# Scan chunk 0 prepared in the last input tile, squares of two chunks added on VectorE, three final additions on POOL

## The chip, the core and the metric

One NeuronCore of a Trainium2 chip. The kernel is one launch; its time is the device time of that launch in microseconds. The engines work side by side and meet only through semaphores: TensorE (PE, matmuls into PSUM), VectorE (DVE), ScalarE (ACT), GpSimd (POOL) and SyncE (SP, which issues the DMAs). An engine takes its instructions in the order written, and one that waits holds up all behind it.

## What is computed

The reference is one layer of a streaming encoder on 1024 prompt tokens and 64 sample tokens (T = 1088 columns), width 1024. A combined projection feeds two head groups: latent attention (8 heads) and an RWKV-7 scan (8 heads, state of 64 x 64 per head). Their outputs are projected together, and a SwiGLU of width 2816 follows. Cut to what the change touches:

```python
def rms_norm(x, g):
    return x * lax.rsqrt(jnp.mean(x * x, axis=-1, keepdims=True) + RMS_EPS) * g

proj = h @ lw['w_in']                          # c_q, c_kv, k_r, rw
q = rms_norm(c_q, lw['q_norm_g']) @ lw['w_uq']
ckv_new = rms_norm(c_kv, lw['kv_norm_g'])
...                                            # attention; scan over r, decay, k, v, kk, a
m = jnp.concatenate([o_attn, o_rw], axis=-1) @ lw['w_out']
x = x + gt_a * rms_norm(m, lw['norm_g'][1])
h = rms_norm(x, lw['norm_g'][2]) * (1 + sc_f) + sh_f
f = (jax.nn.silu(h @ lw['w_gate']) * (h @ lw['w_up'])) @ lw['w_down']
x = x + gt_f * rms_norm(f, lw['norm_g'][3])
```

## The kernel before

Features lie on the 128 partitions, tokens on the free axis, so a row of 1024 features is 8 tiles. The tokens are cut into three chunks `CH` of 364, 364 and 360 columns; the output projection takes them in `OUT_ORDER` = 1, 0, 2. Large projections run as three reduced-precision products (`chunk_product`, L440); attention, scan and norm sums are plain float32. Each engine has its own program, an order written out by hand. Four stages follow one another: input projection (to about 350 us), attention interleaved with the scan (to about 1010), output projection with two norms per chunk (to about 1190), and feed-forward with its final norm.

A norm is split over the engines. ScalarE squares (`norm_squares`, two pieces of four tiles), TensorE adds the eight tiles of squares by eight matmuls with a matrix of ones (`norm_sum`, L478), ScalarE takes the root (`norm_root`, L489), VectorE the reciprocal (`norm_recip`, L495).

**Seam of input projection and attention.** The last input tiles are the latents `ckv` and `cq`. VectorE norms them chunk by chunk (`latent_norm`, L1482), three times "kv", then three times "q". The scan runs over 17 chunks of 64 tokens. A chunk is first prepared: SP loads it (`load_chunk`), VectorE makes running sums of the log decay (`prepare_sums`, L1531), ScalarE their exponentials and a copy (`prepare_scalar`), VectorE two operands of products (`prepare_rows`, L1543 to L1546), POOL the third (`prepare`, L820). Then TensorE multiplies (`products`, L1977), VectorE masks (`causal`, L1554), TensorE transposes (`turns`), and an inversion in six levels follows. `interleave` mixes these slots with the units of attention (`keys`, `query`, `scores`, ...) in a fixed ratio: keys group 0, products, keys group 1, transposes, keys 2 and 3, first level, and so on. The working tiles of chunk 0 (`cum`, `pinc0`, `bk`, ...) share memory with the weight tiles of the input projection, so its preparation comes after the last input matmul. `products` of chunk 0 also waits for the last query root.

**Output projection.** `out_tile(t, n)` makes 16 half-width groups of matmuls for tile n of the t-th chunk (L2241); ScalarE evicts it (`put_m`, L1259). While chunk t is projected, chunk t-1 goes through norm "m", the residual addition (`residual`, L1728 and L1732), norm "n2" and the modulation with its split in two parts (`feed` on VectorE, `affine_split` on ScalarE). TensorE adds the "m" squares behind tile n = 0 and the "n2" squares behind n = 4. `OUT_PARTS` says behind which eviction ScalarE takes the root of n2 and the split.

**End.** Per chunk, ScalarE squares, scales 8 or 16 pieces by the gain (L1375) and takes the root; VectorE (`finish`) multiplies a half by the reciprocal root (L1855) and adds it to x (L1856), half by half. SP stores each half.

Of the kernel before, what the change touches and what calls it, by code (L numbers as in the profile page):

```python
# [21 lines left out]
P = 128  # L22
# [28 lines left out]
OUT_ORDER = [1, 0, 2]  # L51
LEVELS = 6
Y_EARLY = 12
OUT_PARTS = {3: "n2 root", 7: "split"}
# [143 lines left out]
def build(nc, d):  # L198
    with ExitStack() as ctx:
# [3 lines left out]
        def place(start, *tensors):  # L203
# [49 lines left out]
        cum, pinc0, pneg, bk, ar0, vv, gm0, tt0, xt, bktm0, uv, st0, st1, rhs, end = place(  # L253
            WA, ("cum", [P, PAIRS, C + 1]), ("pinc0", [P, PAIRS, C + 1]), ("pneg", [P, PAIRS, C]), ("bk", [P, PAIRS, 2 * C]),
            ("ar0", [P, PAIRS, 2 * C]), ("vv", [P, PAIRS, 2, C]), ("gm0", [P, 2, PAIRS, 2 * C]),
            ("tt0", [P, 2, PAIRS, C]),
            ("xt", [P, PAIRS, C]), ("bktm0", [P, PAIRS, P]), ("uv", [P, PAIRS, P]), ("st0", [P, PAIRS, DH]), ("st1", [P, PAIRS, DH]),
            ("rhs", [P, PAIRS, C]))
# [14 lines left out]
        ci0, ci1, yb0, yb1, vz0, vz1, ar1, bktm1, pr0, pr1, spr, pt, pinc1, aw, end = place(  # L273
            MIX_AT, ("ci0", [P, SF, PAIRS, C]), ("ci1", [P, SF, PAIRS, C]), ("yb0", [P, PAIRS, C]), ("yb1", [P, PAIRS, C]),
            ("vz0", [P, PAIRS, P]), ("vz1", [P, PAIRS, P]), ("ar1", [P, PAIRS, 2 * C]), ("bktm1", [P, PAIRS, P]),
# [8 lines left out]
        yt, x2a, x2b, s0, s1, m1, *w_late, end = place(  # L284
            R2, ("yt", [P, KR, T]), ("x2_0", [P, KD, 364]), ("x2_1", [P, KD, 364]), ("sq2_0", sq), ("sq2_1", sq), ("m1", [P, KD, 364]),
            ("wo5", tile), ("wo6", tile), ("wo7", tile))
        x2, sq2 = [x2a, x2b], [s0, s1]
# [50 lines left out]
        root_ready, rstd_ready = sem("root_ready"), sem("rstd_ready")  # L338
# [41 lines left out]
        x3_in, scaled, y_done, stored = sem("x3_in"), sem("scaled"), sem("y_done"), sem("stored")  # L380
# [88 lines left out]
        def norm_sum(pe, name, sqbuf, c):  # L469
            k, _ = NORMS[name]  # L470
            n, q = CH[c][1], norm_no[name, c]
            if q >= 2:
                pe.wait_ge(root_ready, q - 1)
            for j in range(-(-k // 4)):
                piece = first_piece[name, c] + j
                pe.wait_ge(sq_ready, piece + 1)
                for i in range(4 * j, min(4 * j + 4, k)):
                    mm = nc.tensor.matmul(ps[:, 6 + q % 2, 0:n], ones, sqbuf[piece % 2][:, i - 4 * j, 0:n], start=(i == 0), stop=(i == k - 1))  # L478
                mm.then_inc(sq_used, 1)

# [76 lines left out]
        def _(sp):  # L557
# [73 lines left out]
            load_chunk(1, 1)  # L631
# [130 lines left out]
            for c, (a, n) in enumerate(CH):  # L762
                for j in range(2):
                    sp.wait_ge(y_done, 2 * c + j + 1)
                    sp.dma_start(d["y"].rearrange("(k p) t -> p k t", p=P)[:, 4 * j:4 * j + 4, a:a + n],
                                 x3[:, 4 * j:4 * j + 4, a:a + n]).then_inc(stored, 16)
# [6 lines left out]
        def _(pool):  # L773
# [33 lines left out]
            for u in range(2):  # L807
                pool.wait_ge(out_ready[u], 3 * OUT_M)
            nc.gpsimd.memset(state[0][:, :, :], 0.0).then_inc(state_ready, 1)
# [75 lines left out]
            prepare(0, 0)  # L885
            pool.wait_ge(krope_sent, 16)
# [14 lines left out]
            nc.gpsimd.memset(acc[:, :, :], 0.0).then_inc(acc_zero, 1)  # L901


        @block.scalar
        def _(act):
# [175 lines left out]
            for c in range(3):  # L1081
                put_chunk(CQ_AT + 2, c, latent(cq, 2, c))
                act.wait_ge(bank_free[1], 3 * (OUT_M - 1) + c + 1)
                act.wait_ge(bank_free[0], 3 * OUT_M)
                norm_squares(act, "q", cols_of(cq, c), sq_lat, c)
                if c:
                    norm_root(act, "q", c - 1)
            for u in range(2):
                act.wait_ge(out_ready[u], 3 * OUT_M)
            act.wait_ge(krope_put, 1)  # L1090
            for e in range(2):
                nc.scalar.copy(kt[e][64:96, 0:T], krope[64:96, :]).then_inc(krope_copied, 1)
            norm_root(act, "q", 2)

            def prepare_scalar(f, u):
# [8 lines left out]
                nc.scalar.copy(vv[:, :, :, :], cin[u][:, 5, :, :].unsqueeze(2).broadcast_to([P, PAIRS, 2, C])).then_inc(c_v, 1)  # L1104

# [139 lines left out]
            prepare_scalar(0, 0)  # L1245
# [120 lines left out]
            for c, (a, n) in enumerate(CH):  # L1366
# [6 lines left out]
                parts = [(k, b, w, s) for k in range(KD) for b, w, s in segments(c)]  # L1373
                for i, (k, b, w, s) in enumerate(parts):
                    ins = nc.scalar.mul(acc[:, k, b:b + w], acc[:, k, b:b + w], gains[:, 3, k, s:s + 1])  # L1375
                    if i < len(parts) - 1:
                        step.mark(ins)
                    else:
                        ins.then_inc(scaled, 1)
                norm_root(act, "f", c)  # L1380
# [3 lines left out]
        def _(dve):  # L1384
# [138 lines left out]
            for c in range(3):  # L1523
                latent_norm("q", cq, KQ, V_QG, c)

# [76 lines left out]
            def slot_vector(s, u):  # L1602
# [10 lines left out]
                causal(s, u)  # L1613
                yield
# [126 lines left out]
            def feed(t):  # L1741

                c = OUT_ORDER[t]
                a, n = CH[c]
                norm_recip(dve, "n2", c)
# [124 lines left out]
        def _(pe):  # L1870
# [564 lines left out]
```

## Time and profile before

| what | us |
|---|---|
| median of 3 runs | 2007.57 (1996.54 to 2008.99) |
| the profiled execution, its own time | 2004.83 |
| its span (first to last instruction) | 2001.9 |
| TensorE busy in the span | 1880.9 (94%) |
| VectorE busy | 964.6 (48%) |
| ScalarE busy | 625.7 (31%) |
| POOL busy | 339.3 (17%) |

The rows below come from that one execution; times in them are microseconds from the start of the span. A bracket at the end of a timeline row is the idle time of the engine before it and what ended it. Rows that belong together are merged into one, with their count; a plain float32 matmul counts twice, since it runs in two passes.

### The profile page before, as it was taken

The page shows a single profiled execution, that of the slowest core. Times are in us where ns is not written, and L with a number is a line of the kernel's source. Part 1 is how long each engine was busy: PE and PEld are TensorE (multiplying, and loading weights), DVE is VectorE, ACT ScalarE, POOL GpSimd, SP SyncE. Part 2 cuts the span into 40 slices and gives each one's busy share as a digit, 9 for nine tenths or more (in the row PEclk, how much of TensorE's full clock was granted, in tenths as well). Part 3 has the DMA queues.
Part 4 walks back from the last instruction along what each step waited for, and adds up shares of the span by engine and source line. Part 5 has one row for each costly group of instructions (what it writes and reads, how often), then busy time and mean ns, then how long its engine had stood idle before and what let it go on. Part 6 is the DMA issues. An engine that isn't in the chain of part 4 may idle for free. (4 is left out here: it accounts for less than half of the span.)

```text
span 2001.9 us, 42614 instructions
## 1 busy us (share of the span) xinstructions
PE 1880.9 (94%) x17546; PEld 1592.2 (80%) x17546; DVE 964.6 (48%) x1538; ACT 625.7 (31%) x1260; POOL 339.3 (17%) x408
## 2 busy tenths in 40 slices
PE   5999999799999999998999999999999999999996
PEld 3888889377667667666744489999999999999995
DVE  4597675645554554555404362342342342342347
ACT  4644433244334443434422242111011012012114
POOL 0032320225435335335410010000000000000000
PEclk9899999899999998999999999999999999999998
DMA  8357774010110110102040222121021011021032
GB/s 332 107 167 199 195 184 155 21 52 26 50 39 27 50 39 26 49 26 83 21 150 31 80 83 72 34 64 43 23 64 43 23 64 53 12 64 53 11 121 89
DMA packets 126184, 151.30 MB, mean 76 GB/s; under 512 B 83152, under 2 KB 98128, under 8 KB 125552
## 3 DMA queue, kind: packets, MB, share of 16 engines
q1 hardware_dynamic: 126000, 148.56, 23.8%
q8 instruction: 150, 2.46, 0.5%
q14 instruction: 34, 0.28, 0.0%
HBM read 118.05 MB, written 30.50 MB: 74 GB/s over the span
## 5 line engine op out<-in xcount | busy, mean ns | idle before, releaser
L440 PE MATMUL ps<-fhi,whi 128*128 128x364 f32 (+1 forms) x1056 | 350.0, 331 | 14.3 <-issue 8.0
L440 PE MATMUL ps<-flo,whi 128*128 128x364 f32 (+1 forms) x1056 | 347.5, 329 | 0.0
L440 PE MATMUL ps<-fhi,wlo 128*128 128x364 f32 (+1 forms) x1056 | 346.4, 328 | 0.0
L432 DVE TENSOR_TENSOR wlo<-wraw,whi 128x1024 fp32r<-128x1024 f32 x70 | 86.6, 1238 | 276.4 <-ACT whi L428 273.6
L440 PEld LDWEIGHTS ps<-fhi,whi 128*128 128x128 f32 x1056 | 198.9, 188 | 16.8 <-issue 13.3
L440 PEld LDWEIGHTS ps<-fhi,wlo 128*128 128x128 f32 x1056 | 199.7, 189 | 0.0
L440 PEld LDWEIGHTS ps<-flo,whi 128*128 128x128 f32 x1056 | 199.1, 189 | 0.2
L440 PE MATMUL ps<-hhi,whi 128*128 128x364 f32 (+1 forms) x480 | 167.8, 350 | 11.2 <-DVE hlo L1399 10.9
L1820 DVE TENSOR_TENSOR acc<-acc,ps 128x364 f32<-128x364 f32 (+1 forms) x240 | 126.5, 531 | 101.9 <-PE ps L2266 101.8
L833 POOL TENSOR_TENSOR nlev<-gm,con 64x256 f32<-64x256 f32 x204 | 154.8, 759 | 119.5 <-DVE gm L1554 105.5
L2266 PE MATMUL ps<-ahi,dhi 128*128 128x364 f32 (+1 forms) x480 | 158.6, 330 | 2.4 <-DVE acc L1820 2.4
L440 PE MATMUL ps<-hlo,whi 128*128 128x364 f32 (+1 forms) x480 | 158.8, 331 | 0.0
L440 PE MATMUL ps<-hhi,wlo 128*128 128x364 f32 (+1 forms) x480 | 158.8, 331 | 0.0
L2266 PE MATMUL ps<-alo,dhi 128*128 128x364 f32 (+1 forms) x480 | 157.5, 328 | 0.0
L2266 PE MATMUL ps<-ahi,dlo 128*128 128x364 f32 (+1 forms) x480 | 157.3, 328 | 0.0
L1305 ACT ACTIVATE sil<-ps 128x364 f32<-128x364 f32 (+1 forms) x60 | 27.3, 471 | 342.4 <-PE ps L440 342.4
L1572 DVE TENSOR_TENSOR tt<-tt,ps 128x512 f32<-128x512 f32 (+1 forms) x85 | 53.9, 634 | 140.1 <-PE ps L2011 117.3
L440 PEld LDWEIGHTS ps<-hhi,whi 128*128 128x128 f32 x480 | 91.2, 190 | 18.9 <-issue 15.1
L1451 DVE SCALAR_TENSOR_TENSOR scr<-late,cond 128x1024 f32<-128x1024 f32 x64 | 96.8, 1513 | 14.3 <-DMA late<-in_ada_t 12.3
L2109 PE MATMUL ps<-kt,qt 96*64 96x512 f32 (+8 forms) x512 | 90.7, 472 | 6.9 <-DVE qt L1693 6.9
L2266 PEld LDWEIGHTS ps<-ahi,dhi 128*128 128x128 f32 x480 | 90.1, 188 | 5.8 <-DVE acc L1820 5.6
L440 PEld LDWEIGHTS ps<-hlo,whi 128*128 128x128 f32 x480 | 91.3, 190 | 3.2
(235 smaller groups left out, 3225.3 us busy)
## 6 DMA issues: line engine op xcount, KB each, us to landing
wraw<-in_w_tiles SPq DMA_DIRECT2D x68, 512.0 KB, 4.5
late<-in_ada_t SPq DMA_DIRECT2D x32, 512.0 KB, 3.8
ci<-scan SPq DMA_DIRECT2D x17, 768.0 KB, 4.4
draw<-in_w_down SPq DMA_DIRECT2D x20, 512.0 KB, 3.6
slab<-in_ada_w SPq DMA_DIRECT2D x4, 2048.0 KB, 17.7
x<-in_x_t SPq DMA_DIRECT2D x4, 1456.0 KB, 10.1
bg<-bg SPq DMA_DIRECT2D x17, 256.0 KB, 2.8
x<-x_mid SPq DMA_DIRECT2D x1, 4352.0 KB, 13.1
```

What stands on the lines that cost most here:

```text
L432: nc.vector.tensor_tensor(wlo[u][:, :, :], wraw[u][:, :, :], whi[u][:, :, :].bitcast(F32), ALU.subtract).then_inc(w_lo, 1)
L440: mm = nc.tensor.matmul(ps[:, 3 * u + c, 0:n], w[u][:, k, :], x[:, k, :], start=(k == 0 and i == 0), stop=(k == KD - 1 and i == 2))
L833: nc.gpsimd.tensor_tensor(nlev[r, l, :, :], gm[u][r, e, :, 0:C], lv, ALU.mult).then_inc(c_lev, 1)
L1305: nc.scalar.activation(sil[c][:, 0:n], ps[:, c, 0:n], ACT.Silu).then_inc(sil_ready, 1)
L1451: nc.vector.scalar_tensor_tensor(out=scr[:, :], in0=late[t % 2][:, :], scalar=1.0, in1=cond[s][:, :], op0=ALU.mult, op1=ALU.mult, accum_ou ...
L1572: nc.vector.tensor_tensor(t2, t2, ps[:, WB, 0:n * PAIRS * C], ALU.add).then_inc(c_tev, 1)
L1820: nc.vector.tensor_tensor(acc[:, k, a:a + n], acc[:, k, a:a + n], ps[:, 6 + x % 2, 0:n], ALU.add).then_inc(d_added, 1)
L2109: mm = nc.tensor.matmul(ps[64 * e:64 * e + 64, 2 * (x % 2) + b, 0:n], qt[e][0:96, q0:q0 + C], kt[e][0:96, k0:k0 + n], start=True, stop=True)
L2266: mm = nc.tensor.matmul(ps[:, 6 + x % 2, 0:n], w[u][:, P * k:P * k + P], y[slot][:, u, a:a + n], start=(u == 0 and w is dhi and y is ahi), ...
```

## The change

Three edits, with the memory plan that they need.

1. The tiles of chunk 0 move to memory that is free during the last input tiles (after `wait_spilled`), and its whole preparation moves there: on ScalarE ahead of the last `cq` evictions, on VectorE between the "kv" and the "q" norms, on POOL ahead of the wait for the last input matmul. `ci1`, the buffer of chunk 1, moves the other way, so its load comes behind the last input matmul on SP. The query norm of chunk 2 goes into slot 0 behind the mask; ScalarE takes the last query root ahead of two copies of rope keys.
2. For the first two chunks of `OUT_ORDER`, the squares of a norm lie in one buffer. VectorE adds the eight tiles by one `tensor_reduce` (with a step of 364 elements from tile to tile), and TensorE sums the partitions with a single matmul, placed one tile later (behind n = 1 and n = 5). `OUT_PARTS` becomes 4 and 6.
3. `finish` does both multiplications first, and three of the last four additions go to POOL. ScalarE takes the root between the two halves of its scaling, and signals each half.

```diff
+POOL_ADDS = [(1, 0), (1, 1), (2, 0)]
-OUT_PARTS = {3: "n2 root", 7: "split"}
+OUT_PARTS = {4: "n2 root", 6: "split"}
...
+        def tile_sum(dve, name, c):
+            i, n = SUMMED.index((name, c)), CH[c][1]
+            assert first_piece[name, c] % 2 == 0
+            dve.wait_ge(sq_ready, first_piece[name, c] + 2)
+            if i:
+                dve.wait_ge(sq_used, first_piece[SUMMED[i - 1]] + 2)
+            nc.vector.tensor_reduce(square_sum[:, 0:n], sq_all[:, :, 0:n].rearrange("p k n -> p n k"), AX_X, ALU.add).then_inc(sum_ready, 1)
+        def summed_norm(pe, name, c):
+            i, n, q = SUMMED.index((name, c)), CH[c][1], norm_no[name, c]
+            pe.wait_ge(root_ready, q - 1)
+            pe.wait_ge(sum_ready, i + 1)
+            nc.tensor.matmul(ps[:, 6 + q % 2, 0:n], ones, square_sum[:, 0:n], start=True, stop=True).then_inc(sq_used, 2)
...
             load_chunk(0, 0)
-            load_chunk(1, 1)
...
             for u in range(2):
                 sp.wait_ge(out_ready[u], 3 * OUT_M)
+            load_chunk(1, 1)
...
             prepare(0, 0)
+            for u in range(2):
+                pool.wait_ge(out_ready[u], 3 * OUT_M)
+            pool.wait_ge(c_k, 2 + 1)
+            nc.gpsimd.memset(state[0][:, :, :], 0.0).then_inc(state_ready, 1)
...
+            for i, (c, j) in enumerate(POOL_ADDS):
+                (a, n), h = CH[c], slice(4 * j, 4 * j + 4)
+                pool.wait_ge(y_rms, 2 * c + j + 1)
+                if i:
+                    pool.wait_ge(y_added, i)
+                nc.gpsimd.tensor_tensor(x3[:, h, a:a + n], x3[:, h, a:a + n], acc[:, h, a:a + n], ALU.add).then_inc(y_added, 1)
...
+            prepare_scalar(0, 0)
+            for c in range(3):
+                put_chunk(CQ_AT + 2, c, latent(cq, 2, c))
...
+            norm_root(act, "q", 2)
+            for u in range(2):
+                act.wait_ge(out_ready[u], 3 * OUT_M)
+            act.wait_ge(krope_put, 1)
+            for e in range(2):
+                nc.scalar.copy(kt[e][64:96, 0:T], krope[64:96, :]).then_inc(krope_copied, 1)
...
             for c in range(3):
                 latent_norm("kv", ckv, KKV, V_KVG, c)
-            for c in range(3):
-                latent_norm("q", cq, KQ, V_QG, c)
...
                 causal(s, u)
+                if isinstance(s, int) and s == 0:
+                    latent_norm("q", cq, KQ, V_QG, 2)
...
-            dve.wait_ge(state_ready, 4)
+            dve.wait_ge(state_ready, 3)
             prepare_sums(0, 0)
             prepare_rows(0, 0)
+            for c in range(2):
+                latent_norm("q", cq, KQ, V_QG, c)
...
+                if t < 2:
+                    tile_sum(dve, "m", c)
                 norm_recip(dve, "m", c)
...
-                dve.wait_ge(scaled, c + 1)
-                for j in range(2):
-                    h = slice(4 * j, 4 * j + 4)
-                    step.done(nc.vector.tensor_tensor(acc[:, h, a:a + n], acc[:, h, a:a + n], over_tiles(rstd[:, a:a + n], 4), ALU.mult))
-                    nc.vector.tensor_tensor(x3[:, h, a:a + n], x3[:, h, a:a + n], acc[:, h, a:a + n], ALU.add).then_inc(y_done, 1)
+                halves = [slice(0, 4), slice(4, 8)]
+                for j, h in enumerate(halves):
+                    dve.wait_ge(scaled, 2 * c + j + 1)
+                    nc.vector.tensor_tensor(acc[:, h, a:a + n], acc[:, h, a:a + n], over_tiles(rstd[:, a:a + n], 4), ALU.mult).then_inc(y_rms, 1)
+                for j, h in enumerate(halves):
+                    if (c, j) not in POOL_ADDS:
+                        dve.wait_ge(y_rms, 2 * c + j + 1)
+                        nc.vector.tensor_tensor(x3[:, h, a:a + n], x3[:, h, a:a + n], acc[:, h, a:a + n], ALU.add).then_inc(y_done, 1)
...
-                    if t and n == 0:
+                    if t and n == 1:
...
-                        norm_sum(pe, "m", sq2, OUT_ORDER[t - 1])
-                    if t and n == 4:
-                        norm_sum(pe, "n2", sq2, OUT_ORDER[t - 1])
+                        summed_norm(pe, "m", OUT_ORDER[t - 1])
+                    if t and n == 5:
+                        summed_norm(pe, "n2", OUT_ORDER[t - 1])
```

## Rows read from the trace of the kernel before

**Rows 1.** The page: busy time by engine; then the chain by line

```profile
PE 1880.9 (94%) x17546; PEld 1592.2 (80%) x17546; DVE 964.6 (48%) x1538; ACT 625.7 (31%) x1260; POOL 339.3 (17%) x408
...
PE ps L440 25%; PE ps L2266 11%; PE ps L2327 1%; PE ps L478 1%; DVE wlo L432 1%; DVE acc L1820 0%; DVE rstd L495 0%; DVE acc L1855 0%; DVE x L1856 0%; ACT x L956 0%; DVE x L1732 0%; DVE x L1748 0%; DVE sil L1758 0%; ACT sq L467 0%; ACT fhi L961 0%
```

**Rows 2.** Timeline, TensorE, seam (start, us, what, [idle before])

```profile
347.36 3.99 PE L478 MATMUL ps<-sq_lat,con 128*128 128x364 f32 x12
351.28 1.44 PE L2159 MATMUL ps<-ckv,aw 128*64 128x364 f32 x8
362.31 2.08 PE L1977 MATMUL ps<-ar,bk 64*128 64x128 f32 x16 [9.58 <-DVE bk L1546]
364.31 2.69 PE L2159 MATMUL ps<-ckv,aw 128*64 128x364 f32 x8
```

**Rows 3.** Stretches of the seam: busy by engine, granted clock, DMA

```profile
361.00:365.00 4.00, 2.69 (x20) 2.13 (x22) 2.21 (x4) 0.00 (x0) 0.43 (x1) 0.50 0.40 127
```

**Rows 4.** Timeline of VectorE, then of ScalarE, at the seam

```profile
344.16 2.43 DVE L495 RECIPROCAL rstd<-rstd 128x364 f32<-128x364 f32 x1 [10.53 <-ACT rstd L489]
...
357.94 0.83 DVE L1531 TENSOR_TENSOR_SCAN cum<-con,ci 128x64 f32<-128x64 f32 x4
359.56 0.42 DVE L1543 TENSOR_TENSOR ar<-ci,pinc 128x256 f32<-128x256 f32 x1 [0.79 <-ACT pneg L1102]
...
333.75 0.46 ACT L999 COPY cq<-ps 128x360 f32<-128x360 f32 x1 [3.53 <-PE ps L440]
337.74 0.46 ACT L999 COPY cq<-ps 128x364 f32<-128x364 f32 x1 [3.54 <-PE ps L440]
...
343.56 0.56 ACT L489 ACTIVATE rstd<-ps,con 128x364 f32<-128x364 f32 x1 [0.23 <-PE ps L478]
...
349.39 0.56 ACT L489 ACTIVATE rstd<-ps,con 128x364 f32<-128x364 f32 x1 [0.24 <-PE ps L478]
```

**Rows 5.** Timeline of TensorE in the output projection

```profile
1051.08 2.67 PE L2241 MATMUL ps<-oatt,wo 128*64 128x364 f32 x16
...
1070.80 5.16 PE L478 MATMUL ps<-sq,con 128*128 128x364 f32 x16
...
1097.84 6.82 PE L478 MATMUL ps<-sq,con 128*128 128x364 f32 x16 [2.20 <-ACT sq L467]
...
1144.49 0.44 PE L440 MATMUL ps<-fhi,whi 128*128 128x364 f32 x1 [0.56 <-ACT m L1259]
...
1150.97 5.08 PE L478 MATMUL ps<-sq,con 128*128 128x360 f32 x16 [2.20 <-ACT sq L467]
```

**Rows 6.** Timeline of ScalarE in the output projection

```profile
1041.70 2.72 ACT L467 ACTIVATE sq<-m 128x1456 f32<-128x1456 f32 x2
```

**Rows 7.** Groups by line and shape, VectorE, then POOL: count | busy, mean ns

```profile
L495 DVE RECIPROCAL rstd<-rstd 128x364 f32<-128x364 f32 x12 | 29.1, 2426 | 74.0 <-ACT rstd L489 74.0
...
L1659 DVE TENSOR_REDUCE sm<-ps 128x1 f32<-128x1024 f32 x4 | 4.9, 1225 | 11.4 <-PE ps L2109 11.4
...
L801 POOL TENSOR_TENSOR aa<-aa,kk 128x1089 f32<-128x1089 f32 x4 | 10.1, 2513 | 64.0 <-DVE kk L1467 64.0
```

**Rows 8.** Timeline of POOL, then of VectorE, where both read two tiles

```profile
255.96 3.36 POOL L796 TENSOR_TENSOR k_row<-k_row,tmp 128x1089 f32<-128x1089 f32 x1
259.39 3.41 POOL L799 TENSOR_TENSOR tmp<-r_row,k_row 128x1089 f32<-128x1089 f32 x1
...
256.99 3.41 DVE L1451 SCALAR_TENSOR_TENSOR scr<-late,cond 128x1024 f32<-128x1024 f32 x1
```

**Rows 9.** Timeline of TensorE, VectorE and ScalarE at the end

```profile
1979.81 5.08 PE L478 MATMUL ps<-sq,con 128*128 128x360 f32 x16 [0.17 <-ACT sq L1371]
...
1982.58 1.68 DVE L1855 TENSOR_TENSOR acc<-acc,rstd 128x1456 f32<-128x1456 f32 x1
...
1996.56 1.66 DVE L1856 TENSOR_TENSOR x<-x,acc 128x1440 f32<-128x1440 f32 x1
...
1987.13 0.54 ACT L489 ACTIVATE rstd<-ps,con 128x360 f32<-128x360 f32 x1
```

More of the change, by code:

```diff
@@ L250, in build @@
         sq_lat = [sl0, sl1]
[L253 to L258, printed above, removed]
+        gm0, tt0, xt, bktm0, uv, st0, st1, rhs, ci1, yb0, bktm1, end = place(
+            WA, ("gm0", [P, 2, PAIRS, 2 * C]), ("tt0", [P, 2, PAIRS, C]), ("xt", [P, PAIRS, C]), ("bktm0", [P, PAIRS, P]), ("uv", [P, PAIRS, P]),
+            ("st0", [P, PAIRS, DH]), ("st1", [P, PAIRS, DH]), ("rhs", [P, PAIRS, C]), ("ci1", [P, SF, PAIRS, C]), ("yb0", [P, PAIRS, C]),
+            ("bktm1", [P, PAIRS, P]))
         state = [st0, st1]
@@ L272, in build @@
         assert end <= R2
-        ci0, ci1, yb0, yb1, vz0, vz1, ar1, bktm1, pr0, pr1, spr, pt, pinc1, aw, end = place(
-            MIX_AT, ("ci0", [P, SF, PAIRS, C]), ("ci1", [P, SF, PAIRS, C]), ("yb0", [P, PAIRS, C]), ("yb1", [P, PAIRS, C]),
-            ("vz0", [P, PAIRS, P]), ("vz1", [P, PAIRS, P]), ("ar1", [P, PAIRS, 2 * C]), ("bktm1", [P, PAIRS, P]),
+        ci0, cum, pinc0, pneg, bk, ar0, vv, yb1, vz0, vz1, ar1, pr0, pr1, spr, pt, pinc1, aw, end = place(
+            MIX_AT, ("ci0", [P, SF, PAIRS, C]), ("cum", [P, PAIRS, C + 1]), ("pinc0", [P, PAIRS, C + 1]), ("pneg", [P, PAIRS, C]),
+            ("bk", [P, PAIRS, 2 * C]), ("ar0", [P, PAIRS, 2 * C]), ("vv", [P, PAIRS, 2, C]), ("yb1", [P, PAIRS, C]),
+            ("vz0", [P, PAIRS, P]), ("vz1", [P, PAIRS, P]), ("ar1", [P, PAIRS, 2 * C]),
             ("pr0", [P, TP]), ("pr1", [P, TP]), ("spr", [P, SKEYS]), ("pt", [P, RING, 4 * P]), ("pinc1", [P, PAIRS, C + 1]),
@@ L282, in build @@
         past, _ = place(PAST_AT, ("past", [P, KKV, PAST]))
[L284 to L287, printed above, removed]
+        yt, x2a, x2b, sq_all, m1, *w_late, square_sum, end = place(
+            R2, ("yt", [P, KR, T]), ("x2_0", [P, KD, 364]), ("x2_1", [P, KD, 364]), ("sq2", [P, KD, 364]), ("m1", [P, KD, 364]),
+            ("wo5", tile), ("wo6", tile), ("wo7", tile), ("square_sum", [P, 364]))
+        x2, sq2 = [x2a, x2b], [sq_all[:, 0:4, :], sq_all[:, 4:8, :]]
         assert end <= PAST_AT
@@ L379, in build @@
         krope_copied = sem("krope_copied")
-        x3_in, scaled, y_done, stored = sem("x3_in"), sem("scaled"), sem("y_done"), sem("stored")
+        x3_in, scaled, y_rms, y_done, y_added, stored = sem("x3_in"), sem("scaled"), sem("y_rms"), sem("y_done"), sem("y_added"), sem("stored")
         def start_at_one(eng, *sems):
@@ L479, in norm_sum @@
                 mm.then_inc(sq_used, 1)
+        SUMMED = [(name, c) for c in OUT_ORDER[:2] for name in ("m", "n2")]
+        def tile_sum(dve, name, c):
[10 more added lines that the diff above has]
+            nc.tensor.matmul(ps[:, 6 + q % 2, 0:n], ones, square_sum[:, 0:n], start=True, stop=True).then_inc(sq_used, 2)
         def norm_root(act, name, c):
@@ L763, in _ @@
                 for j in range(2):
-                    sp.wait_ge(y_done, 2 * c + j + 1)
+                    if (c, j) in POOL_ADDS:
+                        sp.wait_ge(y_added, POOL_ADDS.index((c, j)) + 1)
+                    else:
+                        sp.wait_ge(y_done, sum((c, j) >= x and x not in POOL_ADDS for x in itertools.product(range(3), range(2))))
                     sp.dma_start(d["y"].rearrange("(k p) t -> p k t", p=P)[:, 4 * j:4 * j + 4, a:a + n],
@@ L806, in _ @@
             nc.gpsimd.memset(sm[:, Y_POW:Y_POW + PAIRS], -0.5).then_inc(pow_ready, 1)
-            for u in range(2):
-                pool.wait_ge(out_ready[u], 3 * OUT_M)
-            nc.gpsimd.memset(state[0][:, :, :], 0.0).then_inc(state_ready, 1)
             nc.gpsimd.memset(cum[:, :, 0:1], 0.0).then_inc(state_ready, 1)
@@ L1080, in _ @@
                 put_chunk(CQ_AT + 1, c, latent(cq, 1, c))
-            for c in range(3):
[L1082 to L1093, printed above, removed]
             def prepare_scalar(f, u):
@@ L1372, in _ @@
                 act.wait_ge(sq_ready, first_piece["f", c] + 2)
[L1373 to L1380, printed above, removed]
+                for half in range(2):
+                    parts = [(k, b, w, s) for k in range(4 * half, 4 * half + 4) for b, w, s in segments(c)]
+                    for i, (k, b, w, s) in enumerate(parts):
+                        ins = nc.scalar.mul(acc[:, k, b:b + w], acc[:, k, b:b + w], gains[:, 3, k, s:s + 1])
+                        if i < len(parts) - 1:
+                            step.mark(ins)
+                        else:
+                            ins.then_inc(scaled, 1)
+                    if half == 0:
+                        norm_root(act, "f", c)
         @block.vector
@@ L1522, in _ @@
                 latent_norm("kv", ckv, KKV, V_KVG, c)
-            for c in range(3):
-                latent_norm("q", cq, KQ, V_QG, c)
             def prepare_sums(f, u):
@@ L1744, in feed @@
                 a, n = CH[c]
+                if t < 2:
+                    tile_sum(dve, "n2", c)
                 norm_recip(dve, "n2", c)
```

10 lines of the change are left out of this document (8 added, 2 removed).

## The prediction

> **What bounds the kernel now.** I read the page first: TensorE is busy for 94% of the span and VectorE for 48% [rows 1]. The chain that ended last is made of TensorE matmuls almost everywhere, so VectorE or ScalarE work costs time only where TensorE stands still for it. A change can help in three ways: fewer matmuls, fewer stands, a shorter stretch behind the last matmul. The diff does one of each, in three stages, and I read each stage in the timeline by engine.
>
> At the seam between input projection and attention, TensorE ends its last norm sum at 351.3, does one group of key matmuls, and stands 9.58 us for VectorE's `bk` [rows 2]. In that stand the granted clock falls to 1.2 GHz (0.50) [rows 3]: the same key matmuls (L2159) take 2.69 us there and 1.44 us before the stand [rows 2]. VectorE meanwhile divides and scales the query latents (until 358), and only then prepares scan chunk 0, from 357.94 until TensorE is released at 362.3 [rows 2, 4].
>
> In the output projection TensorE goes from tile to tile, 19.7 us for four (1051.1 to 1070.8) [rows 5]. Between tiles it spends 5.1 us on each sum of eight squares. The third sum had to wait 2.20 us for ScalarE's squares, the clock was down, and it took 6.82 us; the fifth waited 2.20 us again [rows 5].
>
> At the end, VectorE alone is left from about 1980 on: a reciprocal, two multiplications and two additions for each of two chunks [rows 9].
>
> **The seam.** Removed from the wait: the query norms of chunks 0 and 1 now come behind the preparation, and chunk 2's behind the first causal mask. The preparation moves to about 333.7, where VectorE has nothing to do until 344.2 [rows 4]. It costs four scans (0.83), ScalarE's two exponentials and a copy, and four products against POOL's two (from 359.56 to 362.2 before): some 5 us, finished near 338.5, with 5 us to spare. ScalarE must do its share between the evictions of 333.75 and 337.74 [rows 4]; with its 1.28 us table load that ends at 336.8. The square root then needs a table load of its own, so query root 0 comes at 344.7 and not 343.56 [rows 4]; VectorE ends norms 0 and 1 at 354.05 as before, because root 1 at 349.39 sets that [rows 4]. The second chunk's load moves on SP behind the last projection matmul (347.6) and ahead of the rope keys and the state; it is wanted at 392, so it is hidden by 40 us. POOL's zeroing of the state is moved behind its products; nobody waits.
>
> So the products (L1977) can start at 352.7, behind the first keys, and not at 362.3: 9.6 us. Without the stand I take the clock to stay up, and products and second keys (4.8 us at half clock) cost half: another 2.0 to 2.4, I take 2.0. Against it, the transposes wait for the causal mask, which VectorE can start only at 354.6 (norm 1, one key copy) and ends at 355.9, 0.7 us after TensorE would be ready. Norm 2 (4.0 us: 2.40 + 1.60) then holds VectorE until 359.9; key copies queue behind it, but the fifth key group needs only the first copy, and the first inversion step is due at 361. Sum: 9.6 + 2.0 - 0.7 = 10.9 us less. Bounds: 0 if the stand only moves to a later wait, 12 if nothing waits.
>
> **The sums of squares.** Four of the six sums (m and n2 of the first two chunks) become one VectorE reduction and one matmul pair. By the row of eight, one costs 5.1/8 = 0.6 us. Removed from TensorE: 3 x (5.1 - 0.6) + (6.8 - 0.6) = 19.7 us. Each sum is placed one tile later (behind tile 1 and 5), so I laid out the stage again with tiles of 4.9 us. First m sum: squares ready at 1044.4 [rows 6], reduction to 1047.6, TensorE there at 1050.9. First n2 sum: 1068.0 against 1071.1. Second m sum: ScalarE's split starts at 1078.1, its squares end at 1086.6, reduction to 1089.8, TensorE there at 1091.2, so the 2.20 us stand goes. Second n2 sum: 1108.3 against 1111.3. The last m sum finds its squares ready too: another 2.20. One stand grows: the last eviction now sits behind the split on ScalarE, so the first feed-forward product waits until 1124.0 for a projection that ended at 1121.6, 2.35 us where it was 0.56 [rows 5]. Sum: 19.7 + 2.2 + 2.2 - 1.8 = 22.3, I take 22. Behind it the residual and feed of the last chunk (1156 to 1190) keep their own chain and only start earlier.
>
> The unknown is the reduction: 2912 elements read with a step of 364 elements. No row has such a read. From below it is the contiguous reduction, 1.225 us for 1024 [rows 7], so 3.2 us for 2912; from above the slowest per element on VectorE, the reciprocal (2.426 us for 364), so 19.4 us. I take 3.2, because it is the same operation. The slacks of the layout are 3.1, 3.0, 1.4 and 3.0; at a time R above 6.3 all four are spent and the loss is 4R - 23.3. At 6.4 it is still about 2 us.
>
> The Trainium skill speaks against this edit: SBUF — State Buffer, section "Door 1: The DMA port swizzle", says that an access which crosses to a new 16-byte line pays a penalty, and every element here does. It gives no price; by the row the sum stays at -22, by the rule it is some part of the second rival below.
>
> **The end.** POOL takes both additions of chunk 1 and the first of chunk 2. A POOL operation of 1089 elements takes 2.51 us alone [rows 7], so 1456 take 3.3, twice VectorE's 1.67. What matters is that the two don't run side by side: VectorE's two-input operation of 1.22 us, issued at 256.99 while POOL was in its own (to 259.32), took 3.41 us and ended 1.08 us behind it; POOL's next then took 3.41 instead of 2.51 [rows 8]. They take turns. So from 1984.25, when POOL's first addition is released: VectorE's multiplication to 1985.85, POOL to 1989.0, multiplication 1990.55, POOL 1993.7, multiplication 1995.25, POOL 1998.4, VectorE's own addition 1999.95. Only the reciprocal (2.40) runs beside POOL. Before, the last addition ended at 1998.22 [rows 9]. ScalarE's earlier root (PE's sum ends at 1984.9, before it came at 1987.13 behind sixteen scalings) is in time but buys nothing, since the shared turns set the end. Cost: +1.8 us. Bounds: -4 if the engines ran side by side (POOL would end at 1994.2), +4.2 if the reciprocal takes turns as well. No row has a reciprocal beside POOL.
>
> On that last point the Trainium skill (SBUF — State Buffer, "Who interferes with whom") names only VectorE operations with two SBUF inputs or in a two-port mode, so by it the reciprocal is free and the sum keeps +1.8; the other reading would make it +4.2.
>
> **Sum.** -10.9 - 22 + 1.8 = -31.1. The profiled execution took 2004.83 us with a span of 2001.9; so 1973.7, say 1974. The median of the runs before, 2007.57, is 0.14% above that execution, and the runs spread from 1996.5 to 2009.
>
> **Rivals.**
> First, the seam's gain is swallowed: attention and scan are interleaved in a fixed order, and norm 2 sits on VectorE in slot 0, so keys or inversion could wait instead. For it: TensorE still stands here and there for VectorE in attention. Against: the stands after 352 are short and relative to TensorE's own pace. Time: 1974 + 11 = 1985.
> Second, on the other side: the strided reduction is slow. At four times the contiguous cost (12.8 us) the loss is 4 x 12.8 - 23.3 = 28 us, 2002; at the reciprocal's rate (19.4) it is 54, 2028. It eats all gains (31) from R = 13.6 us on. For it: nothing in the trace reads like this. Against: all VectorE rows but the reciprocal run near one element per 1.05 ns.
> Third, POOL and VectorE overlap at the end: 1974 - 5.8 = 1968. Against it stand [rows 8]; for it, that only a few pairs of such operations are seen.
> Fourth, the output projection gives half: TensorE stands longer before the first feed-forward product or at the last chunk's norms, where nothing was removed. Time: 1974 + 11 = 1985.
>
> **Chances.** Forecast 0.56; seam swallowed 0.14; half of the projection's gain 0.12; overlap at the end 0.08; slow reduction 0.10, of which 0.05 near 2002 and 0.05 above. The range runs from 1963 (overlap, and a fast execution: the lowest before was 8 us under the profiled one) to 1990 (1985 with the reciprocal in turns and a reduction of 6.4) and leaves out the slow reduction and a little more. About 1%, 20 us, is what a measurement of this kernel can tell from no change. Faster than 1987.5: the first four cases less those that add up or land high, 0.80. Same: 0.15. Slower: 0.05.
>
> **What the profile after would show.** Right: L1977 starts near 352.7 with almost no idle before it and full clock there; four `square_sum` reductions of about 3.2 us; matmuls on `square_sum` without a wait; feed-forward starting about 33 us sooner; at the end POOL and VectorE operations of 3 to 5 us that interleave, last addition about 15 us after the last multiplication of chunk 1 began. Wrong: reductions over 6.3 us with TensorE waiting for `square_sum`; a stand of several us in 353 to 372; multiplications of 1.67 us under POOL's additions.

## The result, and the profile after

| | median, us | lowest to highest | ratio to the kernel before | 95% interval |
|---|---|---|---|---|
| before | 2004.66 | 1996.54 to 2008.99 (4 runs) | | |
| after | 1972.96 | 1968.66 to 1981.83 (4 runs) | 0.9848 | 0.9806 to 0.9891 |
| before, in a later job | 2001.42 | 1998.63 to 2006.61 (9 runs) | | |
| after, in that job | 1976.07 | 1974.07 to 1978.37 (4 runs) | 0.9866 | 0.9847 to 0.9885 |

The change makes the kernel 1.3 to 1.5% faster. The profiled execution took 1972.70 us with a span of 1970.9, which is 31.0 less than the span before.

To see where the time went I cut each span at the same five places of TensorE's timeline: the start of the last query norm sum, the start of the fifth key group (the second with `past`), the end of the ninth output tile, the start of the last chunk's "m" sum, and the start of the last norm sum. Where a single sum of squares follows the tenth tile, the end of the ninth lies 4.9 us ahead of that sum.

| us | input projection | seam | attention and scan | output projection | feed-forward | end |
|---|---|---|---|---|---|---|
| before | 347.4 | 24.8 | 673.8 | 105.0 | 828.8 | 22.1 |
| after | 347.8 | 13.4 | 671.1 | 83.9 | 830.5 | 24.2 |
| difference | +0.4 | -11.4 | -2.7 | -21.1 | +1.7 | +2.1 |

The three stages that the diff touches give -30.4 together. The others, where none of TensorE's instructions changed, give -0.6, and they move by several us from one execution to the next (see below).

TensorE at the seam, after. Columns are start, duration, engine and line, operation, and in brackets the idle time before it with what ended it:

```profile
347.80 4.00 PE L478 MATMUL ps<-sq_lat,con 128*128 128x364 f32 x12
351.72 1.44 PE L2200 MATMUL ps<-ckv,aw 128*64 128x364 f32 x8
353.10 1.16 PE L2018 MATMUL ps<-ar,bk 64*128 64x128 f32 x16
354.19 1.45 PE L2200 MATMUL ps<-ckv,aw 128*64 128x364 f32 x8
356.54 0.63 PE L2026 MATMUL ps<-con,bk 128*128 128x128 f32 x4 [0.91 <-DVE gm L1584]
...
361.23 1.94 PE L2200 MATMUL ps<-past,aw 128*64 128x512 f32 x8
```

Against [rows 2]: the products follow the first keys at once, the 9.58 us stand is gone, and the products take 1.16 us where they took 2.08, the second keys 1.45 where they took 2.69. The clock row of the same place says why (duration, busy time of TensorE, weight loads, VectorE, ScalarE and POOL, then the granted clock, DMA share and GB/s); it reads 1.00, 2.4 GHz, where [rows 3] had 0.50:

```profile
353.00:357.00 4.00, 3.09 (x30) 1.95 (x29) 3.94 (x7) 2.42 (x4) 0.37 (x1) 1.00 0.76 244
```

VectorE at the seam, after: the preparation, and then the norms with the mask between them.

```profile
333.99 0.83 DVE L1561 TENSOR_TENSOR_SCAN cum<-con,ci 128x64 f32<-128x64 f32 x4
...
338.93 0.42 DVE L1576 TENSOR_TENSOR bk<-ci,pneg 64x256 f32<-64x256 f32 x1
345.68 2.43 DVE L513 RECIPROCAL rstd<-rstd 128x364 f32<-128x364 f32 x1 [6.33 <-ACT rstd L507]
...
355.11 1.29 DVE L1584 TENSOR_TENSOR gm<-ps,con 128x512 f32<-128x512 f32 x2
356.31 2.39 DVE L513 RECIPROCAL rstd<-rstd 128x360 f32<-128x360 f32 x1
358.74 2.56 DVE L1515 SCALAR_TENSOR_TENSOR cq<-cq,vec,rstd 128x360 f32<-128x360 f32 x3
```

The preparation ends at 339.35, 6.33 us before VectorE is wanted again. The scaling of the last query chunk takes 2.56 us for three instructions; the two before it (364 columns) took 1.62 and 1.61.

TensorE in the output projection, after:

```profile
1037.25 0.88 PE L497 MATMUL ps<-square_sum,con 128*128 128x364 f32 x2
1038.06 2.67 PE L2282 MATMUL ps<-oatt,wo 128*64 128x364 f32 x16
...
1078.96 0.85 PE L497 MATMUL ps<-square_sum,con 128*128 128x364 f32 x2 [0.69 <-DVE square_sum L490]
...
1112.10 0.43 PE L440 MATMUL ps<-fhi,whi 128*128 128x364 f32 x1 [2.14 <-ACT m L1290]
...
1116.21 4.09 PE L478 MATMUL ps<-sq,con 128*128 128x360 f32 x13
```

A sum costs TensorE 0.81 us (1037.25 to the next tile at 1038.06), where eight squares took 5.1 [rows 5]. The 2.20 us stand at the third has shrunk to 0.69, the one at the last "m" sum is gone, and the first feed-forward product waits 2.14 instead of 0.56. VectorE's groups by line and shape (busy us and mean ns of one, then idle time before):

```profile
L490 DVE TENSOR_REDUCE square_sum<-sq 128x364 f32<-128x2912 f32 x4 | 21.9, 5476 | 10.3 <-ACT sq L467 10.3
...
L1893 DVE TENSOR_TENSOR acc<-acc,rstd 128x1440 f32<-128x1440 f32 x2 | 6.9, 3492 | 0.0
L1893 DVE TENSOR_TENSOR acc<-acc,rstd 128x1456 f32<-128x1456 f32 x4 | 6.5, 1672 | 0.1
```

The reduction takes 5.48 us, not 3.2. And the same multiplication line takes 1.67 us for the first two chunks and 3.49 on average for the last (2.28 and 4.70), which runs beside POOL. The end, after:

```profile
1946.75 5.08 PE L478 MATMUL ps<-sq,con 128*128 128x360 f32 x16
...
1951.53 13.74 POOL L932 TENSOR_TENSOR x<-x,acc 128x1456 f32<-128x1456 f32 x3 [788.96 <-DVE acc L1893]
1951.86 0.56 ACT L507 ACTIVATE rstd<-ps,con 128x360 f32<-128x360 f32 x1 [0.23 <-PE ps L478]
...
1952.86 2.40 DVE L513 RECIPROCAL rstd<-rstd 128x360 f32<-128x360 f32 x1
1955.29 6.91 DVE L1893 TENSOR_TENSOR acc<-acc,rstd 128x1440 f32<-128x1440 f32 x2
1962.24 4.55 DVE L1897 TENSOR_TENSOR x<-x,acc 128x1440 f32<-128x1440 f32 x1
```

From its reciprocal at 1947.23 on VectorE has only seven operations, one of them an addition, and still ends 20.0 us behind the start of the last sum (1946.75 to 1966.79), where ten operations ended 18.4 behind it before (1979.81 to 1998.22) [rows 9].

### The profile page after: what moved, and what is told of

It is laid out like the page before. It is cut to its first block and busy times, and to the rows that moved or that the text cites. A ratio compares the mean times of both kernels' runs of the same rounds, so it can differ in the third digit from the quotient of the medians.

```text
span 1970.9 us, 42515 instructions
## 1 busy us (share of the span) xinstructions
PE 1855.2 (94%) x17490; PEld 1577.4 (80%) x17490; DVE 989.1 (50%) x1539; ACT 628.5 (32%) x1262; POOL 352.8 (18%) x411
## 3 DMA queue, kind: packets, MB, share of 16 engines
q1 hardware_dynamic: 126000, 148.56, 24.1%
## 5 line engine op out<-in xcount | busy, mean ns | idle before, releaser
L440 PE MATMUL ps<-hhi,whi 128*128 128x364 f32 (+1 forms) x480 | 167.8, 350 | 11.2 <-DVE hlo L1432 10.9
L932 POOL TENSOR_TENSOR x<-x,acc 128x1456 f32<-128x1456 f32 (+1 forms) x3 | 13.5, 4485 | 789.2 <-DVE acc L1893 789.0
L440 PEld LDWEIGHTS ps<-hhi,whi 128*128 128x128 f32 x480 | 91.1, 190 | 18.9 <-issue 15.1
```

What stands on the lines that cost most here:

```text
L440: mm = nc.tensor.matmul(ps[:, 3 * u + c, 0:n], w[u][:, k, :], x[:, k, :], start=(k == 0 and i == 0), stop=(k == KD - 1 and i == 2))
L932: nc.gpsimd.tensor_tensor(x3[:, h, a:a + n], x3[:, h, a:a + n], acc[:, h, a:a + n], ALU.add).then_inc(y_added, 1)
```

## The edits one by one

**First edit alone, in the kernel before.** The squares and the end are those of before. An excerpt, against the changed kernel:

```diff
-OUT_PARTS = {4: "n2 root", 6: "split"}
+OUT_PARTS = {3: "n2 root", 7: "split"}
...
-                if t < 2:
-                    tile_sum(dve, "m", c)
...
-                    if t and n == 1:
+                    if t and n == 0:
...
-                        summed_norm(pe, "m", OUT_ORDER[t - 1])
...
+                        norm_sum(pe, "m", sq2, OUT_ORDER[t - 1])
...
```

> The kernel before with the first edit alone (preparation of scan chunk 0 in the last input tile, its memory plan, norm 2 in slot 0). Theory (the three edits act in separate stages and add up): the first products start 9.5 us earlier than in before, the fifth key group about 11 us earlier, and the time is 11 us lower, ratio 0.9945. Rival (the gain is swallowed later in attention, and the 34 us of the whole change come from the projection): the fifth key group comes earlier, but the first output tile comes at the time of before, ratio 1.000.

Measured: ratio 0.9949 [0.9921, 0.9976], the seam 13.4 us as in the changed kernel, the end 22.1. The first edit gives the gain at the seam by itself, and most of it lasts: the first output tile starts at 992.52, where it started at 1001.03 before. With the interval of the time (0.2 to 0.8% less) this rules out that the whole gain is lost later in attention. A loss of a few us there could not be told from the scatter of that stage, which took 667 to 677 us in the profiled executions of all kernels here.

**Second edit alone, in the kernel before.** The reverse: only `tile_sum` and `summed_norm` with their places.

> The kernel before with the second edit alone (four sums of squares by a VectorE reduction and one matmul). Theory (adds up): the last sum of m squares comes about 21 us earlier, ratio 0.9895. Reductions of 5.5 us as in the kernel after, one short stand of TensorE below 1 us at the third. Rival (the projection needs the seam's earlier scan): below 15 us, ratio above 0.9925.

Measured: ratio 0.9878 [0.9848, 0.9909]; the seam 24.6 us as before, the output projection 85.4, the third sum again with a stand:

```profile
1084.30 0.85 PE L497 MATMUL ps<-square_sum,con 128*128 128x364 f32 x2 [0.70 <-DVE square_sum L490]
```

**The changed kernel without its third edit.** `finish` and ScalarE's last scaling as in the kernel before, POOL adds nothing:

> The kernel after with its end as in before (all six final additions on VectorE, root behind the scalings). Theory (POOL and VectorE take turns at the end and the third edit costs 2 us): from the start of the last norm sum on TensorE to the end of the span 22.1 us as in before, against 24.2 in the kernel after; total ratio to before about 0.983, 0.1% under the kernel after. Rival (the POOL additions pay, the end of the kernel after is long for another reason): 24 us or more.

Measured: ratio 0.9817 [0.979, 0.9844], and 22.1 us from the last sum's start to the end, where the changed kernel takes 24.2. The interval overlaps that of the changed kernel, so by the times alone the third edit's price is not proven. The stretches show it, because they hardly scatter: 24.1 to 24.2 us in all five profiled executions that end like the changed kernel, 22.1 to 22.2 in the four that end like the kernel before.

The ratios of the first two multiply to 0.9828, beside 0.9817 of the two together: the edits add up.

## Why the seam keeps its gain

The first rival of the prediction was that norm 2 on VectorE makes TensorE wait after all. To see what its place is worth I moved it back ahead of the keys and the mask:

```diff
-                if isinstance(s, int) and s == 0:
-                    latent_norm("q", cq, KQ, V_QG, 2)
...
-            for c in range(2):
+            for c in range(3):
                 latent_norm("q", cq, KQ, V_QG, c)
```

> The kernel after with the query norm of chunk 2 taken out of slot 0 and put behind those of chunks 0 and 1, ahead of the causal mask. Theory (the mask is what TensorE waits for at the seam, so each us of VectorE ahead of it counts): mask 4.0 us later, TensorE's stand before the transposes grows from 0.9 to about 4.9 us, fifth key group 4 us later (less what norm 2 in slot 0 had delayed, 0.65). Rival (TensorE has other work, the place of norm 2 is free): stand and fifth key group unchanged.

Measured: 1977.92 us, one run. TensorE and VectorE in that kernel, then its clock:

```profile
350.99 1.16 PE L2016 MATMUL ps<-ar,bk 64*128 64x128 f32 x16
352.08 1.44 PE L2198 MATMUL ps<-ckv,aw 128*64 128x364 f32 x8
358.39 1.09 PE L2024 MATMUL ps<-con,bk 128*128 128x128 f32 x4 [4.86 <-DVE gm L1584]
359.27 1.06 PE L2026 MATMUL ps<-con,vv 128*128 128x128 f32 x4
360.26 2.06 PE L2198 MATMUL ps<-ckv,aw 128*64 128x360 f32 x8
```

```profile
354.75 1.60 DVE L1515 SCALAR_TENSOR_TENSOR cq<-cq,vec,rstd 128x360 f32<-128x360 f32 x3
```

```profile
357.00:361.00 4.00, 2.61 (x12) 1.95 (x14) 1.78 (x3) 0.64 (x2) 2.30 (x4) 0.64 0.01 2
```

The stand came out at 4.86 as expected, but the seam grew by 5.5 us (18.9 against 13.4), not by 3.4: behind the stand the granted clock is down (0.64 is the mean of a window that begins inside the stand, and over 358.00:361.00 it is 0.53), and transposes and keys take 1.09, 1.06 and 2.06 us instead of 0.63, 0.60 and 1.43. So a stand at this place costs more than its length. It also shows what slowed norm 2 in the changed kernel: here, where POOL isn't yet at work, its three instructions take 1.60 us and not 2.56.

## What the reduction costs, and why

Two theories for 5.48 us: the step of 364 elements between one element read and the next, or something in the reduction itself (eight elements per result, the size). In one kernel I kept the reduction and its size and made the elements of each result neighbours (it adds up other elements, so this kernel leaves out the true sums of squares):

```diff
-            nc.vector.tensor_reduce(square_sum[:, 0:n], sq_all[:, :, 0:n].rearrange("p k n -> p n k"), AX_X, ALU.add).then_inc(sum_ready, 1)
+            nc.vector.tensor_reduce(square_sum[:, 0:n], sq_all[:, :, :].rearrange("p k n -> p (k n)").rearrange("p (n k) -> p n k", k=8), AX_X, ALU.add).then_inc(sum_ready, 1)
```

> The kernel after, with the reduction reading its 2912 elements one behind another, eight neighbours into one result; so the sums of these four norms are those of other elements, and the outputs behind them differ. Theory (the step costs): 3.2 us each as by the contiguous row of before, against 5.5. Rival (eight-element groups cost, not the step): 5.5 us as before.

In the other I replaced it by three plain additions with the same result up to rounding:

```diff
...
-            nc.vector.tensor_reduce(square_sum[:, 0:n], sq_all[:, :, 0:n].rearrange("p k n -> p n k"), AX_X, ALU.add).then_inc(sum_ready, 1)
+            step.done(nc.vector.tensor_tensor(sq_all[:, 0:4, 0:n], sq_all[:, 0:4, 0:n], sq_all[:, 4:8, 0:n], ALU.add))
+            step.done(nc.vector.tensor_tensor(sq_all[:, 0:2, 0:n], sq_all[:, 0:2, 0:n], sq_all[:, 2:4, 0:n], ALU.add))
+            nc.vector.tensor_tensor(square_sum[:, 0:n], sq_all[:, 0, 0:n], sq_all[:, 1, 0:n], ALU.add).then_inc(sum_ready, 1)
...
```

> The kernel after, with the strided reduction (5.5 us) replaced by three additions of halves (four tiles onto four, two onto two, one onto one: 1456, 728 and 364 contiguous elements). Theory (the reduction is long because of its step between elements): 1.7 + 0.9 + 0.5 = 3.1 us together, TensorE's stand of 0.69 at the third sum goes, the last m sum comes 0.7 us earlier against the first output tile. Rival (eight tiles of 364 cost VectorE 5.5 us in any form): 5 us or more, stand unchanged.

VectorE with neighbouring elements:

```profile
1076.54 3.19 DVE L490 TENSOR_REDUCE square_sum<-sq 128x364 f32<-128x2912 f32 x1
```

VectorE with three additions:

```profile
1073.26 1.68 DVE L490 TENSOR_TENSOR sq<-sq 128x1456 f32<-128x1456 f32 x1
1074.97 0.92 DVE L491 TENSOR_TENSOR sq<-sq 128x728 f32<-128x728 f32 x1
1075.92 0.54 DVE L492 TENSOR_TENSOR square_sum<-sq 128x364 f32<-128x364 f32 x1
```

With neighbours as many elements (2912) take 3.19 us, 1.10 ns for one; [rows 7] has 1.20 for one (1225 ns for 1024). So the step is the cause, and it makes the read 1.7 times as long (5.48 against 3.19). The three additions take 3.2 us (1073.26 to 1076.46) and read no more than 1456 elements at a time. In both kernels the stand of 0.69 at the third sum is gone. The times of the single runs (1974.72 and 1976.57 us) are no faster than the changed kernel's, since 0.7 us is far below what one execution differs from the next.

The Trainium skill (SBUF — State Buffer, section "Door 1: The DMA port swizzle") says that each access that crosses to a new 16-byte line pays a penalty. These traces agree as far as they go, for a VectorE read of float32: 1.7 times the time with a step of 364 elements. No run here tried another step, so where the penalty begins is not shown.

## What the end costs, and why

The prediction's mechanism was that POOL and VectorE take turns where both read two operands from SBUF, and that the reciprocal, with one operand, is free. If that is right, a multiplication that takes its second operand from PSUM should be free too. So the last reciprocals are written to PSUM and read there:

```diff
-                norm_recip(dve, "f", c)
+                q = norm_no["f", c]
+                root = ps[:, 6 + q % 2, 0:n] if c else rstd[:, a:a + n]
+                dve.wait_ge(root_ready, q + 1)
+                nc.vector.reciprocal(root, rstd[:, a:a + n]).then_inc(rstd_ready, 1)
+                dve.wait_ge(rstd_ready, q + 1)
...
-                    nc.vector.tensor_tensor(acc[:, h, a:a + n], acc[:, h, a:a + n], over_tiles(rstd[:, a:a + n], 4), ALU.mult).then_inc(y_rms, 1)
+                    nc.vector.tensor_tensor(acc[:, h, a:a + n], acc[:, h, a:a + n], over_tiles(root, 4), ALU.mult).then_inc(y_rms, 1)
```

> The kernel after, with the reciprocal roots of the last two chunks written to PSUM, so that VectorE's four multiplications there read one tile of SBUF and one of PSUM; the three POOL additions stay. Theory (VectorE and POOL take turns only where both read two tiles of SBUF): the multiplications of chunk 2 take 1.6 us each where the kernel after has 6.9 us for two, the three POOL additions take about 3.3 us each (10 us from first to last instead of 13.7), last norm sum to end of span 20 us instead of 24.2. Rival (POOL slows VectorE by any work at all): multiplications still 3 us or more, 24 us.

The end of that kernel:

```profile
1951.05 10.04 POOL L932 TENSOR_TENSOR x<-x,acc 128x1456 f32<-128x1456 f32 x3 [788.44 <-DVE acc L1897]
...
1952.38 2.40 DVE L1892 RECIPROCAL ps<-rstd 128x360 f32<-128x360 f32 x1
1954.82 3.22 DVE L1897 TENSOR_TENSOR acc<-acc,ps 128x1440 f32<-128x1440 f32 x2
1958.07 4.54 DVE L1901 TENSOR_TENSOR x<-x,acc 128x1440 f32<-128x1440 f32 x1
```

The two multiplications of the last chunk take 3.22 us together where they took 6.91, POOL's three additions 10.04 where they took 13.74, all at the same time. The last addition, both operands in SBUF, still takes 4.54: it starts 3.0 us before POOL ends (1961.09) and needs 1.5 behind it. From the last sum's start to the end it is 20.4 us (1946.27 to 1966.7). The Trainium skill has this as a rule (SBUF — State Buffer, "Who interferes with whom"): a VectorE instruction with at most one SBUF input, outside the modes that use both ports, doesn't contend with POOL, and one with two contends with a POOL instruction that reads SBUF. These rows agree on both counts: 3.22 us for two multiplications with one SBUF input, 4.54 for one addition with two.

Next the same with POOL left only the two additions of chunk 1 (`POOL_ADDS = [(1, 0), (1, 1)]`):

> As the one with reciprocals in PSUM, but POOL makes only the two additions of chunk 1 and VectorE both of chunk 2. Theory: POOL is done before VectorE adds, so nothing takes turns; last norm sum to end of span 19 us. Rival: VectorE's own two additions make it as long as with three on POOL.

Measured 19.3 us (1948.61 to 1967.9): POOL now ends at 1960.09, when VectorE comes to its additions, and nothing takes turns any more:

```profile
1957.16 3.22 DVE L1897 TENSOR_TENSOR acc<-acc,ps 128x1440 f32<-128x1440 f32 x2
1960.30 3.22 DVE L1901 TENSOR_TENSOR x<-x,acc 128x1440 f32<-128x1440 f32 x2
```

And the changed kernel with `POOL_ADDS = []`, all on VectorE:

> The changed kernel with all last additions on VectorE, so that of the third edit only ScalarE's earlier root and the order (both multiplications, then both additions) stay. My theory: VectorE has the same ten operations as in the kernel before, back to back, and its last reciprocal waits behind the additions of the chunk before; multiplications and additions of chunk 2 take 1.60 us each, and the stretch from the start of the last norm sum to the end is 22 us, as in the kernel before (22.1), 2 us under the changed kernel's 24.15. The rival, that the earlier root is worth something by itself, expects 20 us.

```profile
1960.62 3.25 DVE L1897 TENSOR_TENSOR x<-x,acc 128x1456 f32<-128x1456 f32 x2
1963.79 2.40 DVE L513 RECIPROCAL rstd<-rstd 128x360 f32<-128x360 f32 x1
1966.22 3.23 DVE L1893 TENSOR_TENSOR acc<-acc,rstd 128x1440 f32<-128x1440 f32 x2
1969.36 3.22 DVE L1897 TENSOR_TENSOR x<-x,acc 128x1440 f32<-128x1440 f32 x2
```

It takes 22.1 us (1954.51 to 1976.6), as in the kernel before. So ScalarE's earlier root is worth nothing by itself. The four ends line up: 24.2 with three additions on POOL in turns, 22.1 without POOL, 20.4 with three on POOL and turns at the last addition alone, 19.3 with two on POOL and no turns.

## The version with both repairs

Three additions instead of the reduction, reciprocals in PSUM, two additions on POOL; beside it the changed kernel once more, in the same job:

> The changed kernel with three edits: the eight tiles of squares are added by three plain additions (4, 2 and 1 tiles) instead of the reduction with a step, the last two reciprocals are written to PSUM and the multiplications read them there, and POOL keeps only the two additions of chunk 1. By my theory (strided read slow, turns only where VectorE reads two operands from SBUF) the three additions take 3.1 us and the stand of 0.69 at the third sum goes, and from the start of the last norm sum to the end it takes 19.3 us where the changed kernel takes 24.15. So some 5.5 us less than the changed kernel in the same job, near 1967 to 1969; against the kernel before 0.982. The rival (the single executions seen of each part were lucky ones) expects a time within 2 us of the changed kernel's.

> The changed kernel itself, once more, on the same chip as the version with three more edits and in five rounds, for the interval. By the first measurement 0.985 of the kernel before, 1971 to 1974. From the start of the last norm sum to the end 24.15 us.

| | median, us | ratio to before | 95% interval |
|---|---|---|---|
| with both repairs | 1966.07 (1964.68 to 1969.01, 5 runs) | 0.9821 | 0.9804 to 0.9838 |
| changed kernel | 1976.07 (1974.07 to 1978.37, 4 runs) | 0.9866 | 0.9847 to 0.9885 |

It beats both kernels. It lies 10 us below the changed kernel where 5.5 were expected, and the changed kernel lies 2 us above the 1971 to 1974 that were expected for it. The third sum of the repaired version has no stand, and its end takes 19.2 us (1947.68 to 1966.9):

```profile
1075.77 0.88 PE L499 MATMUL ps<-square_sum,con 128*128 128x364 f32 x2
```

The repairs account for 5.7 us (5.0 at the end, 0.7 at the third sum). The medians differ by 10, and the ends of the two intervals leave room for 2 to 16. What the rest is stays open; one part that can be seen is the clock. In the profiled executions attention and scan took 670.3 and 676.7 us with the same instructions. The difference lies in two stretches. Each pair of windows holds the same matmuls, first of the version with both repairs, then of the changed kernel in this job:

```profile
359.60:389.60 30.00, 27.38 (x292) 13.56 (x290) 19.64 (x37) 9.03 (x19) 6.82 (x9) 1.00 0.01 2
362.23:395.47 33.24, 30.62 (x293) 14.89 (x290) 19.66 (x38) 9.06 (x19) 6.80 (x9) 0.90 0.01 1
```

```profile
899.00:1029.90 130.90, 122.15 (x1820) 81.76 (x1821) 50.78 (x115) 46.78 (x116) 44.89 (x63) 0.99 0.31 97
904.90:1038.97 134.07, 126.05 (x1820) 84.87 (x1821) 50.78 (x115) 46.79 (x116) 44.89 (x63) 0.95 0.30 95
```

The stretches are 3.2 us longer each, at a granted clock of 0.90 instead of 1.00 and 0.95 instead of 0.99. The changed kernel itself had 671.1 us and 0.99 in its first profile, so this is no property of the edits. The input projection was 2.6 us longer in the changed kernel as well, and its feed-forward 5.1 shorter.

## Why the prediction was right

1974 was predicted for an execution whose time was 1972.70. The mechanisms of all three stages were right. That the sum met the measured 31.0 within 0.1 is partly luck: the errors of the stages (0.5 more at the seam, 0.9 less in the projection, 0.3 more at the end) and the -0.6 of the stages that nobody touched cancel, and attention and scan alone scatter by up to 10 us. Step by step:

- **The seam, -10.9: measured -11.4.** The products start 5.30 us behind the last norm sum's start (353.10 - 347.80); I had put them 5.34 behind it (352.7 - 347.36). The clock stayed up. The wait for the mask is 0.91 where 0.7 was taken. What the sum left out is the first transposes, which ran at the lower clock before (1.12 us at 366.94) and take 0.63 now. The preparation needs 5.4 us for about 5. One term was mis-sized: norm 2 takes 4.95 us and not 4.0, because its last part runs beside POOL's first work behind the mask. It delays nothing up to the fifth key group, but the key copies and the inversion step queue behind it on VectorE (to 363.71), and TensorE stands for 0.65 us right behind that group, where the kernel before and the one with norm 2 ahead do not:

```profile
363.81 0.68 PE L2041 MATMUL ps<-tt,nlev 64*64 64x64 f32 x16 [0.65 <-issue]
```

So up to the next key group the gain is 10.6 us; the stretches of the table hide this in attention. Each of the kernels with the first edit, but the one with norm 2 ahead, has a seam of 13.4, and the kernel with the first edit alone starts its output projection 8.5 us earlier and is faster by 0.2 to 0.8%. So the rival "seam swallowed" is out as a whole, and the 0.65 us are the part of it that is seen.

- **The sums, -22: measured -21.1 in the profiled execution, -19.6 in others.** The mis-sized term is the reduction, 5.48 us for 3.2. Even for neighbours 3.2 wasn't what the row gives in proportion: 1.225 us for 1024 elements make 3.5 for 2912; that 3.19 was measured later suits the 3.2, but the 1.05 ns for one element that the prediction names is lower than its rows give (1.15 to 1.20 in [rows 7] and [rows 9]). The layout of slacks said what that costs: 2.3 us more on slacks of 3.1, 3.0, 1.4 and 3.0 gives one stand of 0.9 at the third sum, and it was 0.69, at that sum alone. (By the layout's own times the first two slacks are 3.3 and 3.1, which changes nothing here.) The single sum was taken at 0.6 us and is 0.81, so four cost 0.8 more. The third stand therefore gives 1.5 instead of 2.2; the fifth is gone as said; the wait of the first feed-forward product grew by 1.6 for 1.8. That R stayed 0.8 us under the 6.3 at which all four slacks are spent is luck: nothing in the trace before read with a step, and the bounds ran from 3.2 to 19.4. There is luck in the 6.8 us of the third sum too. In the kernel with the first edit alone, whose projection is that of before, the same sum behind the same stand of 2.20 us took 5.13 us, and the stage 103.3 instead of 105.0: 1.7 us of the gain go back to the clock of the one execution that was read.
- **The end, +1.8: measured +2.1.** The turns are as described: multiplications of 2.28 and 4.70 us (3.49 on average), POOL additions of 4.58 (13.74/3), the reciprocal untouched at 2.40. The last addition ends 20.0 us behind the last sum's start, against 18.4, so 1.6 more where I had 1.7. The remaining 0.4 is the last store, which lands 4.1 us behind that addition and 3.7 before.
- **The rivals.** Overlap at the end (1968) fell by the rows of 3.49 us; the slow reduction by 5.48 us, under the 6.3 at which its price begins to run away; half of the projection's gain by the 83.9 to 85.4 us of that stage in all kernels with the reduction as it is (105.0 before, 103.3 with the first edit alone).

What the prediction didn't see is a swing of 1.5 us in the projection. The same stretch from the first feed-forward product to the last chunk's "m" sum takes 4.11 us in some executions (1112.10 to 1116.21) and 5.64 in others (1118.75 to 1124.39 in the changed kernel's second profile). In the latter the granted clock is down behind the stand of 2.14 (0.66 in this window, where the same place of the first profile has 1.00):

```profile
1121.00:1125.00 4.00, 4.00 (x17) 3.77 (x17) 0.56 (x1) 0.43 (x1) 0.00 (x0) 0.66 0.01 4
```

## What to carry to other kernels

When work moves from TensorE to another engine, lay out the slack of each place where it is waited for: a cost that was 1.7 times too low moved the sum by only 0.7 us here, and the layout said so beforehand. An engine that could "help" at the end must be priced with what it does to the other: POOL's additions of 3.3 us cost 2.1 us while they took turns with VectorE, and paid 1.7 (22.1 to 20.4) once VectorE's multiplications read one operand from PSUM, or 2.8 (to 19.3) when POOL kept only two of the three. A stand of TensorE is worth more than its length where the clock falls behind it, so a small edit that keeps it fed can pay twice.

## What I had not expected of the hardware

- A VectorE reduction that reads float32 with a step of 364 elements takes 1.7 times the contiguous one: 5.48 us against 3.19 for 2912 elements.
- After a stand of 4.86 us in the middle of matmuls the granted clock was down (0.53 over 358.00:361.00), as it was after the 9.58 us that stood there before (0.50), though the stand was only half as long. After stands of 2.14 us it fell in some executions of a kernel and not in others (0.66 and 1.00 in a window of 4 us), which is 1.5 us each time.
- POOL and VectorE take turns on small operations as well: in the preparation, with 256 elements, two of VectorE's four took 0.96 and 0.95 us beside POOL's two, the others 0.42.
